# Hidden values of a SwiGLU chunk: one transpose per chunk and a trip through DRAM in place of sixteen transposes

## The reference, cut to what matters

```python
D_MODEL, SEQ, D_FF = 1024, 256, 2816

def swiglu(x, w_gu, w_down):
    g, u = jnp.split(x @ w_gu, 2, axis=-1)
    return (jax.nn.silu(g) * u) @ w_down

def swiglu_ffn(h, w_gate, w_up, w_down):
    return (jax.nn.silu(h @ w_gate) * (h @ w_up)) @ w_down

for l in range(DEPTH):            # first block; the second is alike
    f = swiglu(rms_norm(x, ffn1_pre_g[l]), ffn1_w_gu[l], ffn1_w_down[l])
    x = x + 0.5 * rms_norm(f, ffn1_post_g[l])
    m = hybrid_mixer(rms_norm(x, mix_pre_g[l]), ...)
    x = x + rms_norm(m, mix_post_g[l])
    f = swiglu(rms_norm(x, ffn2_pre_g[l]), ffn2_w_gu[l], ffn2_w_down[l])
    x = x + 0.5 * rms_norm(f, ffn2_post_g[l])
```

## Time and profile before

| | |
|---|---|
| median of 3 runs | 1883.22 us (1882.74 to 1883.33) |
| profiled execution | 1883.3 us, span 1882.0 us |
| TensorE busy | 1873.4 us, 100% of the span, 8974 matmuls |
| weight loads of TensorE | 1572.4 us, 84% |
| VectorE busy | 1574.0 us, 84%, 3072 instructions |
| ACT busy | 1103.4 us, 59%, 1812 instructions |
| granted TensorE clock | 1.0 over the whole span |
| transfers | 350.25 MB, 186 GB/s on the mean |

### The profile page before, as it was taken

One profiled execution on the slowest core, in us unless ns is written; L12 is line 12 of the kernel. 1 busy time (PEld: TensorE's weight loads), 2 busy tenths in 40 slices (PEclk: granted clock), 3 DMA queues, 4 the chain that ended last, 5 costly groups with the idle time before them and its releaser, 6 DMA issues.

```text
span 1882.0 us, 25018 instructions
## 1 busy us (share of the span) xinstructions
PE 1873.4 (100%) x8974; PEld 1572.4 (84%) x8974; DVE 1574.0 (84%) x3072; ACT 1103.4 (59%) x1812; POOL 153.5 (8%) x193
## 2 busy tenths in 40 slices
PE   9999999999999999999999999999999999999999
PEld 7888998888888898888888888888888888888887
DVE  7998789988898868998799878689879987858986
ACT  6554876555655586655555557555555555656553
POOL 1120030000000013000000014100000000500000
PEclk9999999999999999999999999999999999999999
DMA  6765535665666553665466645356655664535653
GB/s 247 238 220 180 197 128 188 217 199 168 199 229 213 168 191 124 201 205 198 160 214 213 204 144 186 113 182 201 201 165 192 212 202 152 180 113 193 206 193 111
DMA packets 97787, 350.25 MB, mean 186 GB/s; under 512 B 10880, under 2 KB 12032, under 8 KB 97408
## 3 DMA queue, kind: packets, MB, share of 16 engines
q1 hardware_dynamic: 95184, 340.13, 54.6%
q10 hardware_dynamic: 2448, 8.53, 1.3%
q0 software_dynamic: 32, 0.00, 0.0%
HBM read 347.57 MB, written 1.05 MB: 185 GB/s over the span
## 4 chain that ended last, share of the span: by engine, by line
PE 94%; DVE 3%; ACT 1%; issue 1%; DMA 0%; SPq 0%; POOL 0%; DVEq 0%; ACTq 0%
PE ps_gu L482 18%; PE ps_gu L480 18%; PE ps_gu L481 18%; PE ps_acc L480 10%; PE ps_acc L482 10%; PE ps_acc L481 10%; PE ps_gu L726 1%; PE ps_gu L727 1%; PE ps_gu L728 1%; PE ps_acc L500 1%; DVE sb_wl L1932 1%; PE ps_gu L1074 0%; DMA sb_scratch<-stream 0%; PE ps_acc L1035 0%; PE ps_tr L480 0%
## 5 line engine op out<-in xcount | busy, mean ns | idle before, releaser
L480 PE MATMUL ps_gu<-sb_wh,sb_xh 128*128 128x512 f32 (+2 forms) x1592 | 620.4, 390 | 0.3 <-DVE sb_wl L1929 0.3
L482 PE MATMUL ps_gu<-sb_wh,sb_xl 128*128 128x512 f32 (+2 forms) x1592 | 617.2, 388 | 0.0
L481 PE MATMUL ps_gu<-sb_wl,sb_xh 128*128 128x512 f32 (+2 forms) x1592 | 616.7, 387 | 0.0
L1257 ACT ACTIVATE sb_wh<-sb_raw,sb_const 128x512 fp32r<-128x512 f32 x344 | 248.2, 721 | 274.6 <-DMA sb_raw<-stream 130.2
L1994 DVE STREAM_TRANSPOSE sb_scratch<-sb_scratch 32x128 f32<-32x128 f32 x1280 | 387.4, 303 | 24.8
L1932 DVE TENSOR_TENSOR sb_wl<-sb_raw,sb_wh 128x1024 fp32r<-128x1024 f32 (+2 forms) x296 | 352.5, 1223 | 23.2 <-ACT sb_wh L1261 20.7
L482 PEld LDWEIGHTS ps_gu<-sb_wh,sb_xl 128*128 128x128 f32 x1592 | 298.9, 188 | 60.0
L480 PEld LDWEIGHTS ps_gu<-sb_wh,sb_xh 128*128 128x128 f32 x1592 | 299.0, 188 | 59.7 <-issue 1.3
L481 PEld LDWEIGHTS ps_gu<-sb_wl,sb_xh 128*128 128x128 f32 x1592 | 299.1, 188 | 58.6
L1261 ACT ACTIVATE sb_wh<-sb_raw 128x1024 fp32r<-128x1024 f32 (+2 forms) x296 | 302.4, 1044 | 64.7 <-DMA sb_raw<-stream 29.6
L1927 DVE SCALAR_TENSOR_TENSOR sb_wl<-sb_raw,sb_const,sb_wh 128x512 fp32r<-128x512 f32 x344 | 257.6, 749 | 90.4 <-ACT sb_wh L1258 90.1
(11 more groups left out here) (279 smaller groups left out, 1580.2 us busy)
## 6 DMA issues: line engine op xcount, KB each, us to landing
sb_raw<-stream SPq DMA_DIRECT2D x620, 512.0 KB, 4.4
sb_raw<-stream SPq DMA_DIRECT2D x8, 416.0 KB, 4.1
sb_raw<-stream SPq DMA_DIRECT2D x8, 390.0 KB, 3.7
sb_scratch<-stream SPq DMA_DIRECT2D x6, 512.0 KB, 8.6
sb_gpost<-post_gains ACTq DMA_DIRECT2D x6, 512.0 KB, 5.2
sb_params<-params ACTq DMA_DIRECT2D x2, 1128.5 KB, 7.7
sb_scratch<-gain_rows ACTq DMA_DIRECT2D x4, 512.0 KB, 5.9
sb_raw<-stream SPq DMA_DIRECT2D x4, 384.0 KB, 3.1
```

Source lines behind the costliest of these rows:

```text
L480: pe.matmul(out, xh, wh, start=start, stop=False)
L481: pe.matmul(out, xh, wl, start=False, stop=False)
L482: return pe.matmul(out, xl, wh, start=False, stop=stop)
L1257: go(m.wh[:, u % RING, 0:512], m.unit(u)[:, 0:512], ACT.Copy, scale=m.gpre[:, e, k:k + 1])
```

## The change

`turn_squares` issues one transpose over all 128 partitions and 512 columns. It turns every square of 32 by 32 in place, that is, within its group of 32 partitions, and writes to a new buffer `squares`. The squares are then moved between the groups by transfers: SP writes `squares` to a scratch in DRAM (`write_squares`, 128 rows of 2 KB), and ACT reads it back with four transfers, one per group of 32 partitions (`read_squares`, 64 KB each, in pieces of 512 bytes). `both_high` waits for the four. `both_high` and `both_low` read `hid_t` through a view with another order of its axes. SP's write stands in its queue behind the load of the unit that is the fourth after the last one VectorE split before the turn. The orders at chunk 0 and in the seams are changed to match.

```diff
@@ Signals, Memory
+        self.squares_out = nc.alloc_semaphore("hidden_squares_written_out")
+        self.squares_back = nc.alloc_semaphore("hidden_squares_read_back")
-        self.hid_t = self.carve(3584, 2, CW)
+        self.squares = self.carve(3072, 4, 4, 32)
+        self.hid_t = self.carve(3584, 4, 4, 32)
+        self.turned_hid = self.hid_t.rearrange("p i b n -> p b i n")
@@ helpers
-def square(a, of_partitions, of_columns):
-
-    blocks = a.rearrange("p t (i n) -> p (t i) n", i=2)
-    return blocks[32 * of_partitions:32 * of_partitions + 32, :, 32 * of_columns:32 * of_columns + 32]
+def quarter(i):
+    return slice(32 * i, 32 * i + 32)
+def trips(f, j):
+    return LAST * f + j + 1
+def turn_after_split(f, j):
+    return FIRST_UNIT[FFN_STAGE[f]] + 8 + 6 * j
+def by_square(a):
+    return a.rearrange("p t (c i n) -> p (t c) i n", c=2, i=4)
@@ ACT
     def both_high(f, j):
-        act.wait_ge(*s.squared.at(squared_count(f, j)))
-        go(m.hh[:, both_places(j), :], m.hid_t, ACT.Copy).then_inc(*s.both_high.up())
+        act.wait_ge(s.squares_back, 64 * trips(f, j))
+        go(by_square(m.hh[:, both_places(j), :]), m.turned_hid, ACT.Copy).then_inc(*s.both_high.up())
+
+    def read_squares(f, j):
+
+        act.wait_ge(s.squares_out, 16 * trips(f, j))
+        if squared_count(f, j) > 1:
+            act.wait_ge(*s.both_low.at(squared_count(f, j) - 1))
+        rows = aps["squares"][trips(f, j) % 2].rearrange("(i u) (j m) -> j u i m", i=4, j=4)
+        for units in range(4):
+            act.dma_start(m.hid_t[quarter(units)].rearrange("p i b n -> p i (b n)"), rows[units]).then_inc(s.squares_back, 16)
@@ ACT, steady
             if j > 1:
                 split(1)
-            both_high(f, j - 1)
-            split(1 if j > 1 else 2)
-            silu(f, j, 0)
+                read_squares(f, j - 1)
+                split(1)
+                both_high(f, j - 1)
+            else:
+                read_squares(f, 0)
+                split(2)
+                silu(f, 1, 0)
+                both_high(f, 0)
+            if j > 1:
+                silu(f, j, 0)
@@ ACT, each seam
         split(1)
+        read_squares(f, LAST - 1)
+        split(1)
         both_high(f, LAST - 1)
-        split(1)
         silu(f, LAST, 0)
@@ VectorE
     def turn_squares(f, j):
 
+        assert at_unit[0] == turn_after_split(f, j), (f, j, at_unit[0])
         for t in range(2):
             vec.wait_ge(*s.hid_done[t].at(11 * f + j + 1))
-        for units in range(4):
-            for tokens in range(4):
-                v = vec.transpose(square(m.hid_t, units, tokens), square(m.hid, tokens, units))
+        blocks = m.hid.rearrange("p t (c j n) -> p (t c) j n", c=2, j=4)
+        if trips(f, j) > 1:
+            vec.wait_ge(s.squares_out, 16 * (trips(f, j) - 1))
+        v = vec.transpose(m.squares.rearrange("p j b n -> p b j n"), blocks)
         v.then_inc(*s.squared.up())
@@ VectorE, steady
             if j > 1:
-                split(1)
-            both_low(f, j - 1)
-            split(1 if j > 1 else 2)
-            hidden(f, j, 0)
+                split(2)
+                both_low(f, j - 1)
+            else:
+                split(2)
+                hidden(f, 1, 0)
+                both_low(f, 0)
+            if j > 1:
+                hidden(f, j, 0)
@@ SP
+    def write_squares(f, j):
+
+        sp.wait_ge(*s.squared.at(squared_count(f, j)))
+        sp.dma_start(aps["squares"][trips(f, j) % 2], m.squares.rearrange("p j b n -> p (j b n)")).then_inc(s.squares_out, 16)
+
+    writes = {turn_after_split(f, j) + RAW: (f, j) for f in range(len(FFN_STAGE)) for j in range(LAST)}
@@ SP, in the loop over units
+        if u in writes:
+            write_squares(*writes[u])
         if u >= EARLY + RAW:
             sp.wait_ge(*s.low_done.at(u - RAW + 1))
         load(u)
+    write_squares(LAST_FFN, LAST - 1)
```

More of the change, by code:

```diff
@@ L1999, in both_low @@
         places = both_places(j)
-        tt(m.hl[:, places, :], m.hid_t, m.hh[:, places, :].bitcast(F32), ALU.subtract).then_inc(*s.both_low.up())
+        tt(by_square(m.hl[:, places, :]), m.turned_hid, by_square(m.hh[:, places, :]).bitcast(F32), ALU.subtract).then_inc(
+            *s.both_low.up())
     def last_low(f, t):
@@ L3118, in declare @@
     aps["positions"] = nc.dram_tensor("positions", (P, 2), I32, kind="ExternalInput").ap()
+    aps["squares"] = nc.dram_tensor("squares", (2, P, 2 * CW), F32, kind="Internal").ap()
     aps["out"] = nc.dram_tensor("out", (P, 2, D), F32, kind="ExternalOutput").ap()
```

## The result

The changed kernel takes 1998.97 us (median of 4 runs, 1996.04 to 2009.28) against 1883.28 for the kernel before on the same chip. The ratio is 1.0624, 95% interval [1.0586, 1.0662]. The sign was forecast, the size was not: +115.7 us, not +13, and outside the range.

The account below looks back on a forecast made before the run. TensorE was taken to bound the kernel at its own pace, so saved VectorE time gives almost nothing; 12.4 us of new waits at chunk 0 on 1883.3 us made 1895.7, said as 1896, range 1885 to 1907.

Parts of the forecast that it names:

- What bounds the kernel, and what goes: TensorE at its own pace; one 0.7 us transpose for sixteen saves VectorE 347 us, worth at most 2.5 us.
- The write: SP's write to DRAM waits behind the load ahead: lands 0.65 us after it, never before 2.95 from the turn's start.
- Issues and reads: ACT's four read issues take 1.6 us (bounds 1.3 and 1.9); each 64 KB read 2.2 to 4.5 us.
- rival B: Reads are slow, 4.5 us each from issue, adding loss at seam and chunk 0; 1907 us, chance 0.15.
- Chunks 1 to 8: Steady chunks: the trip is hidden, high and low parts done by 10.5 us after the turn; no loss.
- cover: Time from the turn's start to TensorE's first down product of the chunk: 15.0 us chunk 8, 10.9 chunk 9, 8.97 to 9.59 chunk 0.
- Chunk 9: At the seam, eight times: low part ready by 175.0, TensorE comes at 175.29; no stall, 0.3 to 1.4 us left.
- Chunk 0: Each FFN's first chunk: write's landing plus 6.5 us overruns; 11.0 us in seven FFNs, 1.4 in the first, sum 12.4.
- A: Not slower: the write lands 2.2 us after issue whatever load is ahead; 1884.8 us, chance 0.15.
- C: A gain: everything is covered and VectorE's saved time shows, at most 2.5 us; 1880.8 us, chance 0.05.

Follow-up runs that it names:

- x9: Changed kernel with chunks 0 and 9 as in the kernel before (sixteen transposes, its orders), chunks 1 to 8 unaltered; 1962.61 us, ratio 1.0427.
- x10: Kernel before, with only chunks 0 and 9 of each FFN by the DRAM trip and the changed orders around them; 1921.65 us, ratio 1.0205.
- x6: Changed kernel with SP's write issued ahead of the two loads that stood before it, except the very first; 1982.55 us, ratio 1.0529.
- x2: Changed kernel without write and reads; copies read the in-place squares directly, the move between partition groups left out; 1882.17 us, ratio 0.9995.
- x11: Changed kernel with two more writes of the squares to spare scratch rows, issued by SP ahead of the real write; 2099.78 us, ratio 1.1152.
- x12: Changed kernel with next chunk's gate activation and hidden product ahead of high and low parts, and write one load earlier; 1937.51 us, ratio 1.032.
- x3: Kernel before with the same five transfers per chunk added, from and to other places, nothing computing waits for them; 1897.97 us, ratio 1.0078.
- x4: Changed kernel with the steady chunks' high and low parts behind the gate's activation and two splits; 1988.41 us, ratio 1.0558.
- x7: Changed kernel with only next chunk's gate activation and hidden product ahead of the steady chunks' high and low parts; 1979.9 us, ratio 1.0514.

## Why the prediction was wrong

- **What bounds the kernel, and what goes.** Right. TensorE didn't wait for the transposes, and 80 transposes take 0.71 us each (0.7 was taken). VectorE's busy time fell by 329 us and not 347: I had counted sixteen transposes from the first start to the last end, 5.04 us, and 0.2 of that is idle time between them; their own is 16 x 0.303 = 4.85. By the groups of the page, before and after (busy us, mean ns, then idle before):

```profile
L1994 DVE STREAM_TRANSPOSE sb_scratch<-sb_scratch 32x128 f32<-32x128 f32 x1280 | 387.4, 303 | 24.8
```

```profile
L2034 DVE STREAM_TRANSPOSE sb_scratch<-sb_scratch 128x512 f32<-128x512 f32 x80 | 56.9, 712 | 8.8 <-issue 1.8
```

- **The write.** Right, and a little low in size. It moves behind the loads, 0.66 us after the later one. In chunks 2 to 8 it lands 5.1 us after the turn's start on the mean (6.3 in the chunk shown above), where the sum had "about 4.7"; in the second FFN's chunk 0 it is 5.46 for 4.65, because the load ahead lands at 4.75 and not at 4.0.
- **Issues and reads.** 1.76 us for four issues in the median and over 2.0 in a tenth of the chunks, near the upper bound of 1.9 and not at 1.6. The reads are the term that was most mis-sized. Their median is 4.6, the end that I kept for rival B. In chunks 2 to 8 they land 4.6 us after the last issue's end, where the sum had 2.7.
- **Chunks 1 to 8: the step that failed.** "Landed by 9, high and low until 10.5; cover 15." The reads landed at 11.6 and the low part was ready at 13.0, still inside 15, and yet it cost 79 us (x9). The cover isn't a constant that the trip may use up: it ends at TensorE's product, but the same trip also delays, by way of ACT's queue, the turn from which the next cover is counted. The room of the loop is TensorE's 16.3 less the 5.5 from the high part to the next turn, 10.8 us from turn to high part. By the prediction's own 9 it would have held with 1.8 to spare; the measured 11.7 didn't. So it took both: the slow reads, and a test that didn't see what their slowness would do. The 15 was also read off chunk 8 alone; in the changed kernel TensorE came to the product of chunks 2 to 8 some 12.3 to 13.3 us after the turn. I named what queues behind ACT's wait only for chunk 0.
- **Chunk 9, "no stall".** Wrong. By itself it loses 7.6 us (x10), which is rival B's size (7): the reads land 10.3 us after the turn on the mean, where the sum had 9.35 at most. Behind the loop it loses 29.5.
- **Chunk 0, 12.4 us.** The mechanism was right, the size low: 21.7, and 23.1 with nothing else late (x10). In the second FFN the trip and chain took 12.7 us for 11.15: 0.8 from the write, 0.8 from what follows its landing, of which the issues were 0.5. The sum had the reads hidden, 3.4 us after the write's landing. In the first FFN and the last three they landed 5.8 to 6.6 us after it, and the high part and the low part right behind it waited for them. The last FFNs have the smallest waits, as said. That the third has the most is right too: these rows are chunk 0 of the second and third, in the changed kernel.

```profile
328.86 0.50 PE L497 MATMUL ps_acc<-sb_wh,sb_fr 128*128 128x512 f32 x1 [3.63 <-DVE sb_fr L2040]
...
528.34 0.79 PE L497 MATMUL ps_acc<-sb_wh,sb_fr 128*128 128x512 f32 x1 [3.97 <-DVE sb_fr L2040]
```

- **The clock.** Not in the sum at all. 22 to 24 us.
- **The rivals.** A is out (the changed kernel's write takes 4.3 us behind loads, x6's 2.2 with none), and so is C (even a free trip, x2, gains about 1 us). B came nearest, with slow reads, but has the loop in it no more than the forecast has.

## What to carry to other kernels

Where a kernel is software-pipelined by in-order lists, don't ask of a longer chain only whether it ends before its consumer starts; follow it round until it meets its own next start, and compare the length of that loop with the period of the bound engine. A queue that waits for a transfer before it issues the next one passes the whole latency on to what stands behind it. And at the pipeline's ends the cover is shorter, so a chain that is hidden in the steady part is to be priced there by itself, with the slower clock that followed such waits here.

## What the runs showed of the hardware

- One VectorE transpose of 128x512 in squares of 32 takes 0.71 us; sixteen of 32x128 take 5.04 from the first start to the last end, 4.85 of it busy.
- TensorE's clock fell to its lower level in some stretches that follow a wait. In x10, the 12 us behind the waits of 2.67, 3.66, 3.69, 3.84 and 4.16 us at chunks 0 were granted 0.86, 0.74, 0.86, 0.77 and 0.78; behind those of 0.86, 1.12, 1.78 and 1.98 us 1.00. A stall of 3.7 us thus costs 5 to 7 (3.69 + 0.14 x 12, 3.66 + 0.26 x 12). In x11's steady chunks waits of 1.90, 2.42, 2.74 and 2.92 us were followed by 0.86, 0.87, 0.86 and 0.87, one of 2.09 and one of 2.53 by 1.00, so length alone doesn't decide.
- A 256 KB write takes 2.2 us from issue to landing with no load out on SP's queue (x6), and 2.2 too with one out that was issued 2.5 us earlier (x12). With two out, the later issued 1.2 us before the write, it takes 4.3 and lands 0.66 behind that load (changed kernel, medians).
- The four 64 KB reads on ACT's queue take a median of 2.7 us (x3) to 5.1 (x12). It goes with how many of SP's transfers are still out when the read is issued: in x3 2.5 us with one out (213 reads) and 4.7 with two (103); in the changed kernel 2.0 with none (4), 4.2 with two (88), 4.7 with three (226); in x12 5.1 with three (248). x4 doesn't fit so well: 3.1 with two (271). When the write got quicker (4.5 to 2.2 from x7 to x12), the reads got slower (4.5 to 5.1).
- Some kernels that wait for transfers scatter more: the changed one over 13.2 us in four runs, x12 over 27.6, the kernel before over 1.2 in thirteen. But x11, whose loop is the longest, stayed within 1.6 in four.
